# Output projections of both attention mixers from split parts instead of true fp32

## The reference

```
for i in (0, 1):
    h  = rms(x) * (1 + sc1) + sh1            # also hc from the context y
    # i = 0, even mixer
    o  = concat([fourier_mix(f), window_attention(q, k, v, kc, vc, sink)]) @ w_out
    oc = concat([fourier_mix(fc), ctx_attention(qc, kc, vc, sink)]) @ w_out
    # i = 1, odd mixer (no output for the context)
    o  = neighbourhood_attention(q, k, v, kc, vc, rel_bias) @ w_out
    x  = x + g1 * o
    h  = rms(x) * (1 + sc2) + sh2
    x  = x + g2 * swiglu(h)                  # the same for y in layer 0
x = second_block(x)
```

## Time and profile before

| | us |
|---|---|
| median of three runs | 2321.68 (2320.24 to 2327.10) |
| profiled execution | 2324.39 |
| its span in the trace | 2322.6 |
| PE busy | 2193.8 |
| DVE busy | 1381.2 |
| ACT busy | 894.4 |
| POOL busy | 160.1 |

### The profile page before, as it was taken

The page is one execution under the profiler, slowest core; times in us unless marked ns, Lnnn a source line. Parts: engine busy times, 40 slices in busy tenths (PEclk is TensorE's granted clock), DMA queues, the critical chain, the costliest instruction groups (busy, mean ns, idle before and its releaser), DMA issues.

```text
span 2322.6 us, 36304 instructions
## 1 busy us (share of the span) xinstructions
PE 2193.8 (94%) x13050; PEld 1828.7 (79%) x13050; DVE 1381.2 (59%) x2472; ACT 894.4 (39%) x1399; POOL 160.1 (7%) x249
## 2 busy tenths in 40 slices
PE   6999899999989999999999899987899999999998
PEld 3654488887876658999997578876789999999997
DVE  4544344342269563664777443989766666666666
ACT  3234322222243363434476101128544444444444
POOL 0021000000013030000000000018200000000000
PEclk8999999999989999999999999999999999999999
DMA  8265232322252274555543233430355555555553
GB/s 310 105 217 187 73 104 95 99 95 95 92 146 84 100 245 137 183 179 182 199 148 107 78 126 119 144 120 0 101 189 190 181 190 189 181 190 189 181 190 127
DMA packets 92838, 340.62 MB, mean 147 GB/s; under 512 B 10409, under 2 KB 10436, under 8 KB 92496
## 3 DMA queue, kind: packets, MB, share of 16 engines
q1 hardware_dynamic: 89280, 325.10, 41.3%
q0 software_dynamic: 3472, 14.35, 2.1%
HBM read 338.36 MB, written 1.05 MB: 146 GB/s over the span
## 4 chain that ended last, share of the span: by engine, by line
PE 80%; DVE 12%; ACT 3%; issue 2%; DMA 1%; DVEq 0%; POOL 0%; ACTq 0%; SPq 0%; POOLq 0%
PE bank L768 19%; PE bank L1042 15%; PE bank L1030 13%; PE bank L535 11%; PE bank L795 8%; PE bank L897 3%; DVE main_zone L1498 2%; DVE main_zone L1615 2%; DVE tail_zone L1495 1%; DVE first_w_parts L1501 1%; PE bank L574 1%; DVE main_zone L1501 1%; PE bank L740 1%; PE bank L719 1%; PE bank L728 1%
## 5 line engine op out<-in xcount | busy, mean ns | idle before, releaser
L768 PE MATMUL bank<-act_parts,first_w_parts 128*128 128x512 f32 (+1 forms) x2928 | 559.9, 352 | 20.3 <-DVE act_parts L1498 13.0
L768 PEld LDWEIGHTS bank<-act_parts,first_w_parts 128*128 128x128 f32 x2928 | 475.4, 193 | 101.3 <-issue 19.7
L1042 PE MATMUL bank<-w_parts,a_parts 128*128 128x512 f32 x1536 | 370.5, 392 | 4.4 <-DVE a_parts L1501 3.4
L1501 DVE TENSOR_TENSOR first_w_parts<-weight_ring,first_w_parts 128x1024 fp32r<-128x1024 f32 x166 | 211.6, 1276 | 259.8 <-ACT first_w_parts L1189 259.6
L1501 DVE TENSOR_TENSOR w_parts<-weight_ring,w_parts 128x1024 fp32r<-128x1024 f32 x235 | 286.8, 1221 | 90.5 <-ACT w_parts L1189 90.5
L1042 PEld LDWEIGHTS bank<-w_parts,a_parts 128*128 128x128 f32 x1536 | 282.6, 189 | 59.5 <-issue 5.1
L1030 PEld LDWEIGHTS bank<-n_parts,w_parts 128*128 128x128 f32 x2568 | 322.1, 191 | 8.3
L1189 ACT ACTIVATE w_parts<-weight_ring 128x1024 fp32r<-128x1024 f32 x235 | 248.0, 1056 | 199.4 <-PE bank L1030 159.0
L1030 PE MATMUL bank<-n_parts,w_parts 128*128 128x256 f32 x2568 | 324.6, 283 | 0.0
L1189 ACT ACTIVATE first_w_parts<-weight_ring 128x1024 fp32r<-128x1024 f32 x166 | 175.0, 1056 | 226.4 <-PE bank L768 126.8
L535 PE MATMUL bank<-main_zone,weight_ring 128*128 128x256 f32 (+1 forms) x976 | 242.7, 410 | 1.5 <-DVE main_zone L1674 0.8
(11 more groups left out here) (226 smaller groups left out, 1981.6 us busy)
## 6 DMA issues: line engine op xcount, KB each, us to landing
weight_ring<-in_stream SPq DMA_DIRECT2D x618, 512.0 KB, 3.4
main_zone<-in_rel_bias POOLq DMA_DIRECT2D x6, 512.0 KB, 14.4
main_zone<-in_decay POOLq DMA_DIRECT2D x1, 1536.0 KB, 8.7
main_zone<-in_xT POOLq DMA_DIRECT2D x1, 1024.0 KB, 11.5
main_zone<-in_ctxT POOLq DMA_DIRECT2D x1, 1024.0 KB, 16.0
tail_zone<-in_rel_bias POOLq DMA_DIRECT2D x2, 512.0 KB, 26.6
tail_zone<-in_keysT POOLq DMA_DIRECT2D x1, 1024.0 KB, 5.0
out<-main_zone SPq DMA_DIRECT2D x2, 512.0 KB, 2.6
```

What stands on the lines that cost most here:

```text
L768: mm = pe.matmul(o[:, 0:w], wb[:, hw, k, :], fin[:, hx, k, 0:w], start=(k == 0 and n == 0), stop=(k == DC - 1 and n == 2))
L1042: mm = pe.matmul(acc[n][:, :], ap_[:, e % 3, ha, (n // 2) * P:(n // 2 + 1) * P], wp[(B + b) % PARTS][:, hw, (n % 2) * 512:(n % 2 + 1) * 51 ...
L1501: return dve.tensor_tensor(o, a, b, op)
```

## The change

`ev_out` and `od_out` join the split weights. The new `mixed_out` multiplies them as three products of parts, with the parts in places of their own (`out_w_parts`, `odd_w_parts`, `odd_w_part`). The blocks 0 and 1 are prepared at the end of the attention, the rest while the projection runs, two tiles ahead. The attention's result is written as a high and a low part: in layer 0 to the two halves of `act_parts` (`fin`), in layer 1 with the low part in the 256 columns of the high half that the context would take. The Fourier half of layer 0 goes to a place `FOUR`, and GpSimd splits it in the units 4 to 7. Squares and sums move to other places, since theirs are taken.

```diff
--- before.py
+++ after.py
@@ -66,7 +66,7 @@
 NSLOTS = _at
 
 
-SPLIT = ("ev_in", "ffn_gu0", "ffn_d0", "od_in", "ffn_gu1", "ffn_d1", "w_in2a", "w_in2b", "w_in2c", "w_in2d", "peer")
+SPLIT = ("ev_in", "ev_out", "ffn_gu0", "ffn_d0", "od_in", "od_out", "ffn_gu1", "ffn_d1", "w_in2a", "w_in2b", "w_in2c", "w_in2d", "peer")
 ORD = {}
 KIND = []
 _n = [0, 0]
@@ -113,6 +113,8 @@
 MASKE0 = 30720
 BIAS0 = 26624
 ATT0 = 34816
+FOUR0 = 17408
+OUTP0 = 19456
 COS0 = 40960
 SIN0 = 41472
 MASKO0 = 41984
@@ -201,6 +203,15 @@
                 with nc.sbuf_tensor("ffn_hidden_parts", [P, 2 * FC * T], F32R) as ffn_hidden_parts:
                     with nc.sbuf_tensor("first_w_parts", [P, PARTS * 2 * 1024], F32R) as first_w_parts:
                         pass
+                pass
+            with nc.sbuf_tensor("odd_rows_place", [P, P0 + 16 * T - H0], F32):
+                with nc.sbuf_tensor("odd_w_parts", [P, 4096], F32R) as odd_w_parts:
+                    with nc.sbuf_tensor("odd_w_part", [P, 2048], F32R) as odd_w_part:
+                        pass
+            with nc.sbuf_tensor("act_parts_place", [P, 2 * DC * T], F32R):
+                with nc.sbuf_tensor("even_rows_place", [P, OUTP0 - P0], F32):
+                    with nc.sbuf_tensor("out_w_parts", [P, PARTS * 2 * 1024], F32R) as out_w_parts:
+                        pass
 
         with nc.sbuf_tensor("mixer_rows_place", [P, NP0], F32):
             with nc.sbuf_tensor("n0_parts", [P, 2 * DC * LT], F32R) as n0_parts:
@@ -221,7 +232,10 @@
         fin = act_parts[:, :].rearrange("p (h c n) -> p h c n", h=2, c=DC)
         fhid = ffn_hidden_parts[:, :].rearrange("p (h c n) -> p h c n", h=2, c=FC)
         fwp = [first_w_parts[:, r * 2048:(r + 1) * 2048].rearrange("p (h n) -> p h n", h=2) for r in range(PARTS)]
-        mwp = [w[:, :].rearrange("p (h n) -> p h n", h=2) for w in (mix_w_parts0, mix_w_parts1, mix_w_parts2)]
+        odp = [w.rearrange("p (h n) -> p h n", h=2) for w in (odd_w_parts[:, 0:2048], odd_w_parts[:, 2048:4096], odd_w_part[:, :])]
+        owp = [out_w_parts[:, r * 2048:(r + 1) * 2048].rearrange("p (h n) -> p h n", h=2) for r in range(PARTS)]
+        mwp = [[mix_w_parts1, mix_w_parts2, mix_w_parts0][(r - ORD["w_in2a"]) % PARTS][:, :].rearrange("p (h n) -> p h n", h=2)
+               for r in range(PARTS)]
         n0p = n0_parts[:, :].rearrange("p (h c n) -> p h c n", h=2, c=DC)
         MG = merge_rows[:, :].rearrange("p (c n) -> p c n", c=DC)
         n2p = n2_parts[:, :].rearrange("p (h c n) -> p h c n", h=2, c=DC)
@@ -316,6 +330,9 @@
         pt_ready = sem("probs_transposed")
         pt_copied = sem("probs_transposed_copied")
         o_ready = sem("attention_out_ready")
+        o_hi = sem("attention_out_high_parts")
+        four_hi = sem("fourier_high_parts")
+        four_split = sem("fourier_low_parts")
         o_copied = sem("attention_out_copied")
         act_chain = sem("act_chain")
         dve_chain = sem("dve_chain")
@@ -384,6 +401,7 @@
         out_ready = sem("out_ready")
         out_done = sem("out_done")
 
+        FOUR = view(FOUR0, 4, T)
         X = view(X0, DC, T)
         H = view(H0, DC, T)
         HR = view(HR0, DC, LT)
@@ -398,22 +416,23 @@
         cond = view(CS_0, DC, CONDW)
         first_cols = [bank[b][:, 0:16].rearrange("p (j m s) -> p j m s", j=2, m=4) for b in (7, 4)]
         ada_cols = [bank[7][:, 0:32], bank[7][:, 0:96], bank[7][:, 0:64]]
-        ada_sums = [view(R0 + 1024, 2, 512), view(R0 + 1024, 2, 512), view(SQ10, 2, 512)]
+        ada_sums = [view(R0 + 1024, 2, 512), view(R0 + 1024, 2, 512), view(R0 + 1024, 2, 512)]
         ADA_BANKS = [(0, 1), (6, 7), (6, 7)]
         PR = view(PR0, 44, LT)
 
 
         norms = [
             dict(src=X, n=T, out=H, sq=view(SQ0, DC, T), layer=0, which=0),
-            dict(src=X, n=T, out=H, sq=view(SQ0, DC, T), layer=0, which=1),
+            dict(src=X, n=T, out=H, sq=view(P0, DC, T), layer=0, which=1),
             dict(src=X, n=T, out=H, sq=view(H0, DC, T), layer=1, which=0),
-            dict(src=X[:, :, 0:L], n=L, out=H[:, :, 0:L], sq=view(SQ0, DC, L), layer=1, which=1),
+            dict(src=X[:, :, 0:L], n=L, out=H[:, :, 0:L], sq=view(P0, DC, L), layer=1, which=1),
             dict(src=HR, n=LT, out=view(RAW0, DC, LT), sq=view(H0, DC, LT), gain="gmix"),
             dict(src=HR[:, :, META:LT], n=L, out=N2, sq=view(SQB0, DC, L), gain="gffn"),
         ]
 
 
         meta = view(H0 + DC * LT, DC, META)
+        ADA_LAST = ["ada0a", "ada1a", "ada1b"]
         BEFORE = {1: "ev_out", 2: "ffn_d0", 3: "od_out", 4: "ffn_d1", 5: "w_out2"}
 
         def squared(k, c):
@@ -434,6 +453,7 @@
         mask_o = view(MASKO0, QT, L)
         stat = view(ST0, 4, 2 * UNITS)
         QKN = [5, 16]
+        OUT, OUTP = ["ev_out", "od_out"], [owp, odp]
 
 
         CHUNKS = [[(4 + j, T, j // 4, SQ0 + j * T, R0 + j * T) for j in range(5)],
@@ -478,8 +498,8 @@
                 split, n, name, i = KIND[s - RING]
                 if split:
                     return w_lo, n + 1
-                if name == "ada0a" and KIND[s - RING + 1][0]:
-                    return ada_rows, 1
+                if name in ADA_LAST and KIND[s - RING + 1][0]:
+                    return ada_rows, ADA_LAST.index(name) + 1
                 if KIND[s - RING + 1][0]:
                     return tile_free, TILE[name] + dict(TILES)[name]
                 return blocks_used, n + 2
@@ -624,14 +644,29 @@
                                    rstd[:, 0:w], start=True, stop=True)
                 mm.then_inc(rstd_spread, 1)
 
-            def project_and_sum(name, rhs, w, k, phase=None):
+            def project_and_sum(name, rhs, w, k):
 
                 for m in range(DC):
                     project(name, DC, rhs, w, m, m + 1)
-                    if m == 0 and phase is not None:
-                        ada_turn(phase)
                 norm(k)
                 spread_rstd(k)
+
+            def mixed_out(name, parts, rhs, w, phase):
+
+                for m in range(DC):
+                    wb = split_block(ORD[name] + m, None, parts)
+                    o = bank_of(TILE[name] + m)
+                    for c in range(DC):
+                        for n, (hw, hx) in enumerate(TERMS):
+                            mm = pe.matmul(o[:, 0:w], wb[:, hw, c, :], rhs(hx, c),
+                                           start=(c == 0 and n == 0), stop=(c == DC - 1 and n == 2))
+                            if c == 0 and n == 0:
+                                mm.then_inc(parts_begun, 1)
+                    mm.then_inc(tile_ready, 1)
+                    if m == 0:
+                        ada_turn(phase)
+                norm(2 * phase - 1)
+                spread_rstd(2 * phase - 1)
 
             def fourier():
                 pr = projections[0]
@@ -818,7 +853,8 @@
             fourier()
             v_turn(0, 0)
             attention(0)
-            project_and_sum("ev_out", H, T, 1, 1)
+            pe.wait_ge(four_split, 4)
+            mixed_out("ev_out", owp, lambda h, c: fin[:, h, c, :], T, 1)
             gate_up(0, T)
             down(0, T)
             for j in range(24):
@@ -828,7 +864,7 @@
             for j in range(8):
                 v_turn(1, j)
             attention(1)
-            project_and_sum("od_out", H[:, :, 0:L], L, 3, 2)
+            mixed_out("od_out", odp, lambda h, c: fin[:, 0, c, h * L:(h + 1) * L], L, 2)
             gate_up(1, L)
             down(1, L)
 
@@ -1161,6 +1197,9 @@
                 u0 = l * PAIRS
                 us = pairs(l)
                 for i in range(PAIRS + 2):
+                    if i == PAIRS:
+                        for b in range(PARTS - 1):
+                            high(OUT[l], b, None, OUTP[l])
                     if i < PAIRS:
                         n = keys_of(l, us[i][1])
                         for half in range(2):
@@ -1228,6 +1267,8 @@
             def before_ffn(l):
 
                 for c in range(DC):
+                    if c + PARTS - 1 < DC:
+                        high(OUT[l], c + PARTS - 1, None, OUTP[l])
                     if c == DC - 1:
                         for b in range(PARTS - 1):
                             high(f"ffn_gu{l}", b)
@@ -1254,7 +1295,7 @@
                 if u >= 1:
                     v = u - 1
                     act.wait_ge(f2_ready, v + 1)
-                    act.activation(H[:, v // 2, (v % 2) * L:(v % 2 + 1) * L], bank[2 + v % 2][:, 0:L], ACT.Copy).then_inc(f2_copied, 1)
+                    act.activation(FOUR[:, v // 2, (v % 2) * L:(v % 2 + 1) * L], bank[2 + v % 2][:, 0:L], ACT.Copy).then_inc(f2_copied, 1)
             v_copy(0, 0)
             attention(0)
             ada_copy(1)
@@ -1671,11 +1712,20 @@
                     if 0 <= j < PAIRS:
                         pair, qt = us[j]
                         dve.wait_ge(o_ready, u0 + j + 1)
-                        dve.tensor_copy(H[:, MIXC[l] + pair, qt * P:(qt + 1) * P], bank[4 + j % 2][:, 0:P]).then_inc(o_copied, 1)
```

(17 more changed lines are left out.)

## The result

| | before | after |
|---|---|---|
| median of 8 runs each, us | 2322.99 (2316.50 to 2329.58) | 2310.05 (2307.02 to 2317.31) |
| ratio, 95% interval | | 0.9947 (0.9935 to 0.9960) |
| profiled execution, us | 2324.39 | 2308.85 |
| its span | 2322.6 | 2307.0 |
| PE / DVE / ACT / POOL busy | 2193.8 / 1381.2 / 894.4 / 160.1 | 2176.0 / 1407.9 / 909.2 / 167.4 |

The change makes the kernel 0.53% faster (0.40 to 0.65%), 12.3 us. The forecast of 2308.4 stands on a before of 2321.68 (0.9943).

A forecast was written before the change was run, and what follows sets the result against it. The prediction took a chain of waits mostly through TensorE as the bound. Terms -11.5 + 0.9 (first projection) and -3.3 + 0.6 (second) gave -13.3 us: 2311.1 profiled, 2308.4 against the median, range 2303 to 2318.

The forecast's parts named there:

- The matmuls: Both projections, split products for fp32: 11.5 us less in the first, 4.6 in the second if TensorE sets the pace.
- The DVE step: Attention units: copy becomes copy, wait and subtraction, 0.39 us more DVE work per unit, hidden in idle gaps, cost 0.
- The Fourier half: First attention, units 4 to 7: GpSimd splits a chunk before its scaling, 2.0 us each, hidden with 0.8 to spare.
- The ends of the attentions: Last units of both attentions: preparing parts starts the projections later, +0.9 us in the first, +0.6 in the second.
- The second projection: At 256 columns: gains 3.3 us, not 4.6; low 7 ends at 22.35, last residual starts at about 27.15.
- the circle: Inside the projections: residual, square, high and low part wait in a ring, 3.1 us against TensorE's 2.88 at 256 columns.
- Loads: SP's DMA queue: order kept, releases come earlier, costed at nothing; uncovered, 5.0 us once.
- The port rule: Attention: DVE contends with GpSimd's SBUF reads only with two SBUF inputs, so the new bank-and-tile subtraction is free.
- The rival: Attention: DVE's new subtraction is held until GpSimd's scaling is done, +25 us, net +12, 2333.7 us; chance 0.07.
- The clock rival: Longer attention tails bring a spell of lower clock to each projection, up to 3 us each, 2314 us; chance 0.06.

The follow-up runs named there:

- the circle open: Changed kernel with DVE's low part of block m + 2 after residual m, not before it: second projection's first matmul to last residual 26.42 us, against 26.52.

## Why the prediction was right

- **The matmuls.** Right. L661 makes a tile in 5.44 us at 512 columns (residuals at 245.43, 250.87, 256.31) and in 2.88 at 256. Body 1 was put at 45.7 and is 45.70.
- **The DVE step.** Hidden, as said. It costs 0.32 to 0.33 us of DVE per unit and not 0.39, as the hand-over inside DVE is 0.04 and not 0.11. Idle time left: 0.60 where about 0.5 was expected, and 0.17 where it was 0.1. One more subtraction per unit, 0.21 us, left the distances between units as they were in both attentions.
- **The Fourier half.** Right: 1.96 us for 2.0, copy 0.60 and subtraction 1.27, and 0.9 us to spare in unit 5 for 0.8. Twice the work cost 3.8 us, so this cover is close.
- **The ends of the attentions.** Sign right, size over: +0.55 for 0.9, and +0.33 for 0.6. Mis-sized is ACT's delay: 0.23 us in the first attention and not 0.4, none in the second and not 0.2, since the row of two high parts starts before the recorded end of the copy ahead of it (204.86 against 203.91 + 1.06) and the next copy before theirs. DVE's added pair, 0.32, makes the rest. The low part between the last two units, which the sum had put on the path of the first attention, costs nothing there.
- **The second projection.** The rows follow the path of the sum: last low part, residuals 5 and 6 right behind it, the FFN parts, last residual. The sizes were a little over: residual 5, right behind the last low part, starts 21.93 us after the first matmul (883.05 - 861.12), where the sum had this part end at 22.35, and the last residual starts at 26.52 and not 27.15, so the gain is 3.9 and not 3.3. TensorE waited for no weight part, where 0.3 us was allowed. What was wrong is the reason why not all of the 4.6 us arrive. The sum put it down to the circle, but with the circle open body 2 was only 0.10 shorter. TensorE itself kept 4.5 of its 4.6 us: it ended its tiles 25.13 us after the start (886.25 - 861.12), and 29.61 before (903.35 - 873.74, the row below). What takes 0.6 of them is the chain from residual 6 through the two FFN high and low parts, which is as long as before, 4.19 us. By the circle or by TensorE's tiles, residual 6 comes within 0.1 us of the same moment here, which the prediction did not see; in that the near hit is partly luck.

```profile
903.35 0.99 PE L614 MATMUL bank<-main_zone,small_zone 128*32 128x64 f32 x56
```

- **Loads.** Nothing, as said. The DMA wait in the first attention is in traces of both kernels.
- **The port rule.** The rival had 7 in 100 and didn't come: the new subtraction, with one input in a bank, kept 0.29 us beside the scaling. The Trainium skill, page "SBUF — State Buffer", section "Who interferes with whom", has it so, and the trace agrees. The same subtraction with two tiles did slow, from 0.29 to 0.64, so the rule's other side is shown too. But the rival's price of 25 us was wrong by its duration: with two tiles the hold was 0.35 us beside a scaling, 0.48 beside the split. With 0.60 idle even that would have been hidden in the second attention, and all of it, extra instruction included, cost 0.67 us in the first.
- **The clock rival.** It did not come in after. The spell that it feared for a longer tail was in one trace, 1.43 us for the 3 us that it named, and behind a wait as long as before, so the longer tails did not bring it. In the norms the swing is 0.87 us (norm 2) and 0.92 (norm 1), and not tied to the change.

The sum of my terms, -13.3, stands against -14.4 from the stretches and -12.3 from the runs. The terms that miss it are the second projection (0.6 too little gained) and the two ends (0.6 too much lost); the first projection, -11.5, measured -11.3.

## What to carry to other kernels

Measure a stage from row to row within one trace, and take a second trace of the kernel before: of the 15.6 us between two spans about 1.2 were of the execution alone. A preparation step is free only up to the idle time of its engine in the tightest unit, so look for that unit, and double the step to learn how near the edge is. When a stage gets shorter, look for the chain at its end that doesn't shrink with it: here the FFN parts ahead of the last residual hold 1.4 us; moving that residual ahead of them was not tried.

## What the hardware showed

- A DVE instruction with both inputs in SBUF waits for the GpSimd instruction that is running and gets in before the next: 0.64 and 0.43 us beside a scaling, 0.77 beside a subtraction of 512 columns, for 0.29 alone. GpSimd's scaling of 512 columns grew from 691 to 705 ns on average. The 5.62 us row fits it: it starts at 705.15, within GpSimd's second instruction (704.89 to 709.69), and ends 1.08 us after that one; GpSimd's third took 5.53 us, and its first two 4.59 and 4.80.
- The granted clock fell at different moments around the same idle stretch in two executions of one kernel, 0.87 us for eight small matmuls. In one execution of fourteen it also fell behind a wait of 1.78 us in an attention, which the others passed at 1.00, and cost 1.43 us.
- A dependent pair on DVE follows in 0.04 us from copy to subtraction when the input is a bank and 128 columns wide; on GpSimd, from SBUF and 512 columns wide, in 0.09 (170.24 + 0.60 to 170.93).
